# A two-block transformer kernel on one core: first tiles through token blocks together, a centring matrix in the value turn, one filler stream for the last pair

## What is computed

```python
h = rms_norm(x, norm_mix_g)
proj = h @ w_in
slab = proj[..., :RWKV_COLS]; slab = slab + (shifted(slab) - slab) * mu      # token shift
r, k, v, wd, ad, gd = split(slab)
decay = exp(-exp(-softplus(-(w0 + tanh(wd) @ w2)) - 0.5))
a = sigmoid(a0 + ad @ a2);  g = sigmoid(gd) @ g2
kk = k * k_k / norm_of_head(k * k_k)
y = delta_rule_scan(r, decay, k, v, -kk, kk * a)      # linear in v
y = (y - mean_of_head(y)) * rsqrt(var_of_head(y) + GN_EPS)
mix = (y * lnx_g + lnx_b + bonus(r, k, v)) * g
x = x + concat([mix, memory_attention]) @ w_out
```

## Time and profile before

| | |
|---|---|
| median of 3 runs (1564.57 to 1568.79) | 1567.27 us |
| the profiled execution's own time | 1571.59 us |
| its span, first to last instruction | 1569.8 us |
| mean granted TensorE clock | 0.987 |
| PE busy | 95% of the span |
| DVE / ACT / POOL busy | 52% / 36% / 16% |
| chain that ended last: PE / DVE / ACT / issue | 81% / 9% / 5% / 3% |
| DMA, mean | 81 GB/s |

### The profile page before, as it was taken

How to read it: one execution, slowest core, us unless ns; L and a number is a source line. 1 busy time by engine, 2 the same in 40 slices (tenths; PEclk the granted TensorE clock), 3 DMA queues, 4 the chain that set the end, 5 groups by cost and what they waited for, 6 DMA issues and landing times.

```text
span 1569.8 us, 26697 instructions
## 1 busy us (share of the span) xinstructions
PE 1486.0 (95%) x11374; PEld 1165.1 (74%) x11374; DVE 821.5 (52%) x1275; ACT 561.1 (36%) x931; POOL 257.8 (16%) x183
## 2 busy tenths in 40 slices
PE   6889998887799999999999999999989999999999
PEld 4666766665588888888878876666768888888887
DVE  6556555665455354453564348688564443444343
ACT  6443344445142222221353337554434331222131
POOL 3133332320020000000020002222322220120120
PEclk9999999999999999999999999999999999999999
DMA  6221101120023323232222232221222333232323
GB/s 217 68 69 43 30 29 29 34 77 3 28 81 94 101 87 108 82 106 94 94 83 93 81 101 88 90 82 58 68 81 94 94 94 108 81 108 94 94 84 104
DMA packets 38517, 127.67 MB, mean 81 GB/s; under 512 B 4224, under 2 KB 5248, under 8 KB 38400
## 3 DMA queue, kind: packets, MB, share of 16 engines
q1 hardware_dynamic: 38400, 125.97, 25.5%
HBM read 123.86 MB, written 2.10 MB: 80 GB/s over the span
## 4 chain that ended last, share of the span: by engine, by line
PE 81%; DVE 9%; ACT 5%; issue 3%; POOL 1%; DMA 0%; SPq 0%; POOLq 0%; DVEq 0%; ACTq 0%
PE bank L927 78%; PE bank L1327 1%; ACT Whi L1967 1%; DVE qa L1640 1%; DVE Hlo L1530 1%; ACT slab L2020 1%; PE bank L1042 1%; DVE Wlo L1524 1%; DVE ftmp L1583 1%; DVE slab L1585 0%; DMA x<-in_xT 0%; PE bank L1117 0%; DVE qa L1638 0%; ACT slab L2152 0%; ACT L2071 0%
## 5 line engine op out<-in xcount | busy, mean ns | idle before, releaser
L927 PE MATMUL bank<-Hhi,Whi 128*128 128x512 f32 x912 | 377.8, 414 | 18.1 <-DVE Wlo L1524 10.3
L927 PE MATMUL bank<-Hhi,Wlo 128*128 128x512 f32 x912 | 364.2, 399 | 0.0
L927 PE MATMUL bank<-Hlo,Whi 128*128 128x512 f32 x912 | 362.3, 397 | 0.0
L927 PE MATMUL bank<-Uhi,Whi 128*128 128x512 f32 x736 | 291.3, 396 | 9.5 <-DVE Ulo L1820 4.0
L927 PE MATMUL bank<-Ulo,Whi 128*128 128x512 f32 x736 | 287.3, 390 | 0.0
L927 PE MATMUL bank<-Uhi,Wlo 128*128 128x512 f32 x736 | 287.3, 390 | 0.0
L1967 ACT CAST Whi<-Wraw 128x1024 fp32r<-128x1024 f32 (+1 forms) x216 | 223.2, 1037 | 161.0 <-PE bank L927 147.0
L1524 DVE TENSOR_TENSOR Wlo<-Wraw,Whi 128x1024 fp32r<-128x1024 f32 (+1 forms) x177 | 226.9, 1282 | 99.9 <-ACT Whi L1967 99.8
L927 PEld LDWEIGHTS bank<-Hhi,Whi 128*128 128x128 f32 x912 | 173.4, 190 | 76.3 <-issue 12.7
L927 PEld LDWEIGHTS bank<-Hlo,Whi 128*128 128x128 f32 x912 | 173.2, 190 | 42.1
L927 PEld LDWEIGHTS bank<-Hhi,Wlo 128*128 128x128 f32 x912 | 173.8, 191 | 34.2
(11 more groups left out here) (302 smaller groups left out, 1638.0 us busy)
## 6 DMA issues: line engine op xcount, KB each, us to landing
Wraw<-in_wts SPq DMA_DIRECT2D x208, 512.0 KB, 3.5
bA<-in_biasA SPq DMA_DIRECT2D x12, 256.0 KB, 2.8
Wraw<-in_wts SPq DMA_DIRECT2D x8, 384.0 KB, 3.2
x<-in_xT SPq DMA_DIRECT2D x8, 256.0 KB, 4.4
X<-in_xT SPq DMA_DIRECT2D x2, 1024.0 KB, 7.2
out<-X SPq DMA_DIRECT2D x8, 256.0 KB, 2.1
bB<-in_biasB SPq DMA_DIRECT2D x4, 384.0 KB, 3.0
memX<-in_memT SPq DMA_DIRECT2D x2, 512.0 KB, 7.0
```

The lines of the kernel that those rows point to most:

```text
L927: return e.matmul(o, lhsT, rhs, start=start, stop=stop, skip_group_check=True)
```

## The change

- Start: x blocks drive three tiles at once (`wa`, `gd`, slab k of pair 0), each tile catching up when its weights are there; weight units 1 and 2 are split inside the loop, so the loads of units 3 and 4 (which wait for Wlo of units 0 and 1) stand ahead of x blocks 2 and 3 in SP's order, and the constants go behind x block 5. The sums of squares of x and of the memory move from POOL to DVE. Two of the ring's banks serve as tile banks for the third and fourth tile. The token-shift's second half becomes a step of its own (`shift`), one tile late in the start.
- The sigmoid of `gd` is a Tanh (scale 0.5) on ACT and an affine on POOL.
- Values less their mean: `turn_v` multiplies by the matrix `cent` (identity less the head's mean) instead of transposing; the `mean` step (matmul and DVE subtraction) is gone, `gsq` squares y at once.
- `table(f)`: a 128x1 activation of function f ahead of the wait in `root` (kinds x, f, t) and in `sg`.
- In `ahead`, exponentials come before the key norm's `root`. Of the 256-column tiles (km) the spreading `hn` comes one flush later. In `mem_projections` the memory's `root` comes after the first qm tile.
- The low part Ulo is a step `tlo` after `tg`. Filler rates: pairs 1.5 to 1.35, pair 0 1.1 to 1.05, room after `sb` 0.7 to 1.4.
- Last pair: `inverse(5)`, `states(5)`, `tail(5)` are one main strand with one filler stream at rate 0.93: bonus, `states(4)`, `tail(4)` in turns with all of the memory attention, then the 14 w_out steps. POOL keeps making Wlo till that strand ends.

```diff
-FILL_FRONT, FILL_TAIL = 0.2, 1
-FILL_PAIR = (1.1, 1.5, 1.5, 1.5, 1.5, 0.87)
+FILL_FRONT, FILL_LAST = 0.2, 0.93
+FILL_PAIR = (1.05, 1.35, 1.35, 1.35, 1.35)
...
+    firsts = [tile(kind, key, ("rw", m), "x", range(8))
+              for kind, key, m in (("wa", (18,), 18), ("gd", (19,), 19), ("slab", (0, 1), 6), ("slab", (0, 0), 0))]
+    first_norm = norm(("x",))
     for i in range(8):
         x0.take(("x", i))
         step("xload", i)
-        if i < 2:
+        if i < 3:
             loads(i + 1)
-        if i == 3:
+        if i == 5:
             step("cload")
+        step("x", i)
+        count("Hlo", "x", i)
+        if i < 3:
+            splits(i + 1)
...
+        step("xq", i)
         x0.give(("x", i))
...
+        for n, g in enumerate(firsts[0:3]):
+            for _ in range(i + 1 if i == n else i > n):
+                next(g)
+            if i == 7 and n == 0:
+                splits(4)
+                next(first_norm)
     step("memload")
+    splits(5)
+    for _ in range(4):
+        next(firsts[3])
+    run(first_norm)
+    state["held"] = held = []
+    for n, g in enumerate(firsts):
+        run(g)
+        if n:
+            shift(held[n - 1])
+        if n == 2:
+            splits(6)
+    shift(held[3])
...
         yield next(r)
+        step("exps", p)
+        step("kf", p)
         bank("root", "f", p)
         yield 0.9
-        step("exps", p)
-        step("kf", p)
...
         two("sb", p)
-        yield 0.7
+        yield 1.4
...
     def tail(p):
-        bank("mean", p)
-        yield 1.0
+        step("gsq", p)
         yield 0
         bank("root", "t", p)
...
         bank("tg", p)
+        yield 1.0
+        step("tlo", p)
         count("Ulo", "mix", p)
-        yield 1.0
+        yield 0
...
+    def beside():
+        yield from turns(itertools.chain(bonus(NP - 1), states(NP - 2), tail(NP - 2)), mem_att)
+        step("Xload")
+        for g in outs:
+            yield from spaced(itertools.islice(g, 7), 0.8)
+
+    filler = beside()
+    blend(itertools.chain(inverse(NP - 1), states(NP - 1), spaced(tail(NP - 1), 1)), filler, FILL_LAST)
+    run(filler)
     state["lo"] = "wlo"
...
         def turn_v(p):
             w.wait_ge(S["shift"], N("shift", slab_tile[p, 2]))
-            transposes(("vn", p), lambda cp: v_[:, 128 * cp:128 * cp + 128]).then_inc(S["vn"])
+            b = bank("vn", p)
+            for cp in range(4):
+                x = mm(b[:, 128 * cp:128 * cp + 128], v_[:, 128 * cp:128 * cp + 128], c("cent"), True, True)
+            x.then_inc(S["vn"])
...
+        def token_square(i):
+            if i:
+                w.wait_ge(S["xsq"], i + 1)
+                w.wait_ge(S["xadd"], i - 1)
+                e.tensor_tensor(acc[:], acc[:], ftmp_of(("x", i))[:], ALU.add).then_inc(S["xadd"])
...
+        def table(function):
+
+            w.wait_ge(S["C"], 16)
+            e.activation(spare[:], c("rmseps"), function, scale=1.0)
```

More of the change, by code:

```diff
@@ L186, in make_plan @@
     plan.TC = late = Slots(4)
-    state = {"loads": 0, "splits": 0, "units": 0, "lo": "wlo"}
+    state = {"loads": 0, "splits": 0, "units": 0, "lo": "wlo", "ahead": 1, "held": None}
     pend = []
@@ L212, in unit @@
         state["units"] += 1
-        splits(u + NW - 1)
+        splits(u + state["ahead"])
         return u
@@ L329, in make_plan @@
             ftmp.give(("x", i))
-        step("x", i)
-        count("Hlo", "x", i)
+        step("xq", i)
         x0.give(("x", i))
-        if i == 0:
-            splits(1)
-    splits(2)
-    step("memload")
-    around(tile("wa", (18,), ("rw", 18), "x", range(8)), tile("gd", (19,), ("rw", 19), "x", range(8)),
-           norm(("x",)))
+        for n, g in enumerate(firsts[0:3]):
[4 more added lines that the diff above has]
+                next(first_norm)
+    step("memload")
+    splits(5)
[10 more added lines that the diff above has]
+    shift(held[3])
+    state["held"] = None
+    for t in (2, 3):
+        M.give(("first", t))
+    state["ahead"] = NW - 1
     def mem_norm():
@@ L504, in make_plan @@
     early = turns(normed, rates0())
[L505 removed]
+    weave(itertools.chain(*(spaced(projection(0, i), 2) for i in (2,))), early, 1.5)
     run(early)
@@ L1989, in root @@
             r = N("root", kind, *key)
+            if kind in ("x", "f", "t"):
+                table(ACT.Sqrt)
             w.wait_ge(S["root"], r)
@@ L2050, in evict, with shift @@
                 e.copy(Hhi2[:, x.key[1], :], tmp_of(("sig", t - 1))[:]).then_inc(S["uphi"])
+        def shift(t):
+            kind = tiles[t].kind
+            if kind == "slab":
+                return
+            w.wait_ge(S["shift"], N("shift", t))
+            if kind == "wa":
+                e.activation(WA[0:64, :], WA[0:64, :], ACT.Tanh, scale=1.0).then_inc(S["lora"])
+            else:
+                e.activation(GD[:], GD[:], ACT.Tanh, scale=0.5).then_inc(S["lora"])
         def gained(ver, i):
@@ L2471, in constants @@
     put("ident", np.eye(128))
+    put("cent", np.eye(128) - same / 64.0)
     put("mneg", -1.0 * (s < t))
```

136 lines of the change are left out of this document (65 added, 71 removed).

## The result

The changed kernel takes 1573.11 us (median of 20 runs, 1568.22 to 1577.88), the kernel before 1567.91 us (20 runs, 1563.93 to 1575.59). The ratio is 1.0031, with a 95% interval of 1.0018 to 1.0044: slower by some 5 us, where 22.5 us less were forecast. So the two profiles are as long as each other, and what they show side by side understates the loss by about 5 us; I compare stretches, and leave whole times to the runs.

The account below looks back on a forecast made before the run. PE bounds it, busy 95% of the span; only its idle time ahead of 430.6 us can move. Start 10, pairs 4 and last pair 8.5 give 22.5 us off 1567.3: 1544.8, range 1531 to 1561.

Parts of the forecast that it names:

- (b): Pairs 0 to 4: `tn` comes 1.4 us earlier, so PE's waits for the gate step's product go, 3.9 us off.
- (a): Pairs 0 to 4: four means go (4.0 us) and five turns of v grow (2.5), 1.5 us off.
- (c): Pairs 0 to 4: the wait for `sb`'s last eviction, 8.1 us in five, stays.
- (d): Pairs 0 to 4: requesting Tanh ahead can't cut the decays' waits; `root` behind exponentials costs pair 2 1.4 us.
- The start: Start and memory projections: fourth tile ends at 38 us, memory's root at 54 to 57; 10 us off, bounds 0 and 16.
- The last pair: Pair 5 as one stream without pair 4's and 5's means: 8.5 us off, bounds 14 and -2.
- the net 1.5 of the first part: Last pair, first part: 2 off for the mean, 1.9 for the last level's wait, 2.4 charged for memory attention rounds.
- The second part: Last pair, second half: memory attention rounds and pair 5's mean leave, w_out steps move behind the last wait; 7.0 us off.
- The dense rest: From 430.6 us on: unchanged, only starting earlier or later; a change over 2 us would show the prediction wrong.
- Slower: starved levels: Rival, chance 0.08: with less filler per unit, level steps wait for their evictions, 25 us more, 1570.
- Tables matter: Rival, chance 0.07: the small activations pull each table load out of the wait for the decays, 1538.

Follow-up runs that it names:

- e2: Changed kernel with `ops` one couple of matmul steps earlier, so that it stands ahead of `tn` again: 1561.09 us, 0.9938 of the kernel before.
- e13: Kernel before with one `yield 0` of the tail left out, so the written order becomes `tn`, `ops`, last couple: 1580.42 us, ratio 1.0073.
- e5: Changed kernel with `ops` ahead of `tn` again and Tanh's table requested behind the eviction of `kn`: 1553.59 us, 0.9907 of the kernel before.
- e3: Changed kernel with the request for Tanh's table moved from `sg` to behind the eviction of `kn`: 1563.98 us, 0.996 of the kernel before.
- e6: Kernel before with one 128x1 Tanh activation added behind the eviction of `kn`: 1558.85 us, ratio 0.9951.
- e1: Changed kernel with the tail's yield after `gsq` put back from 0 to 1.0: 1575.9 us, 1.0036 of the kernel before.
- e7: Changed kernel with three unused products of constants ahead of `sb` in pairs 2 to 5, keeping PE busy: 1573.38 us, 1.0032 of the kernel before.
- e10: Changed kernel with the key norm's `root` ahead of the exponentials again: 1570.53 us, 1.0004 of the kernel before.
- e11: Changed kernel with one tile instead of three going along with the x blocks: 1576.41 us, 1.0049 of the kernel before.
- e8: Changed kernel with the last pair written as before, two blends one after the other: 1579.94 us, 1.0063 of the kernel before.
- e4: Changed kernel with the pairs' filler rates and the room after `sb` put back as before: 1569.51 us, 0.9995 of the kernel before.

## Why the prediction was wrong

- **The step that failed** is (b) of pairs 0 to 4: "`tn` now comes ahead of the last couple of matmul steps ..., 3.9 off". It does come ahead of that couple, but of `ops` too, which stood between; I followed the order on PE and counted 1.4 us gained, and did not lay out DVE's queue. There, the three products of `ops` now stand between `tn` and the gate product, POOL's share of `tn` runs beside two of them, and each takes 1.07 us longer. The wait went from 0.98 to 3.26 us instead of to nothing. e2 and e13 put the price at 12 to 13 us, e5 against e3 at 10.4, the waits themselves at 9.2; against the 3.9 of gain, that is a miss of 13 to 16 of the 27.7 between forecast and result. The forecast also gave the pairs' clock no term: PE was to be busy 1.8 us less over pairs 0 to 4 (four means less, 0.45 more for each of five turns), and is busy 3.7 more, at 0.93 where it was 0.96.
- **(a)** The mean's product went, and turns with `cent` take 0.89 us instead of 0.44 (I had 0.5 more). The size held as PE work, but not as a gain: with the mean gone, `root` t waits 0.81 us for ACT's square in each of pairs 1 to 4 (L2200, 3.2 us in all). No pair of before, e6 or e13 has such a wait. So 3.2 of the four means' 4.0 us come back. In e1, where a yield of 1.0 again stands between the square and `root`, the wait is gone, but the time isn't less: others had come in. The prediction took the product's time off and didn't ask what the fillers at its yield of 1.0 had covered.
- **(c)** said that the wait for `sb`'s eviction stays. It fell to 4.1 us, and this was no gain: PE reached it later and at the lower clock (e7, where it is 9.1 again).
- **(d)** held, and was right on both sides. The request for Tanh in place helps nothing: its load stands right behind the cast, and the waits are as long. Pair 2's decays got a load more, 1.99 for 0.51 us; e10 gives 2.6 us for it (not clear of noise), where I had 1.4. What I missed is that the request is worth 8 to 9 us when it is placed where ACT idles (e3, e6). The rule on tanh beside exp in one set, of the Trainium skill ("ScalarE: Activation LUTs"), agrees with both kernels: before, pair 2's decays come behind exponentials without a load; in the changed kernel, no load stands between the loads at 148.45 and 154.10 us, where the decays and the exponentials are. Its price of 2.66 us for a switch, with a drain, did not come up: load and activation take 1.28 and 0.20 us in the rows of e3, one 0.01 us behind the other, and by 2.66 the wait that e10 takes out would have grown by nearly twice the 1.41 that it did (0.58 to 1.99).
- **The start** gave 6.5 of 10. The waypoints were close: the fourth tile ends at 36 (38), the memory's root starts at 55.85 (54 to 57), with a tile before it. The root came 1.8 us later than before (I had 0.8), the spreading of km waits 1.1 (I had 0). I put the rest, 1.4 us, down to the qm tile: the low clock behind the root's wait, which slowed it before, now slows the tile that comes there, so that 24 x 0.23 = 5.5 us went and not 7.6. That would be 2.1, and wasn't tried; the scatter of the starts (82.8 to 84.5) is as large. That the four tiles' gain goes into the wait for the memory's sum (4.39 to 6.11) held, and e11 bears it out by half.
- **The last pair** gave 2.7 of 8.5. That one stream fills holes was right, and e8 gives it 6.8 us, more than the 4.6 that were its part. The term that failed is the net 1.5 of the first part: from the first scores to the wait for the last level it is 3.8 longer (62.1 for 58.3 us). I charged 2.4 for the rounds and nothing for the clock; PE is busy 7.9 more there, at 0.89 for 0.99. The second part is 6.6 us shorter (I had 7.0).
- **The dense rest** is 2.4 us shorter, which passes the 2 us that I had named as a sign of being wrong. Before, PE came to it out of a wait of 4.01 us and was granted 0.59 in the first 4 us; now the wait is 1.46 and the clock there 1.00:

```profile
430.60:434.60 4.00, 4.00 (x11) 3.04 (x12) 2.04 (x3) 1.24 (x2) 0.00 (x0) 0.59 0.00 0
```

```profile
432.70:436.70 4.00, 3.81 (x16) 2.85 (x17) 2.03 (x3) 1.38 (x3) 0.00 (x0) 1.00 0.00 0
```

  That is 4 x 0.41 = 1.6 us. The other three executions with the 4.0 us wait (e6, e8, e13) also have 0.57 to 0.60 there, and take 1136.1 to 1139.0 us for the rest; so what is left of the 2.4 is within the scatter.

- **The rivals.** "Slower: starved levels" had the sign, with 0.08, and not the mechanism: no level step of pairs 1 to 4 shows a wait of 0.5 us or more. "Tables matter" was right that a load can be pulled out of that wait, but not by this change. The changes sum to -6.5 + 11.3 - 2.7 - 2.4 = -0.3 us in the profiles. Of the 5.2 us between the medians, about 5 are the distance of the profiled runs from their medians (3.7 above, 1.6 below), which no stage shows. By the runs, the parts are: order of `tn` and `ops` +12, root behind the exponentials +2.6, single stream -6.8, three tiles instead of one -3.3. That is +4.5, near the 5.2; but each part is known to some 2 to 4 us only, so the sum proves little. The products less the mean, the squares' additions on DVE and `hn` one flush later were not tried alone.

## What to carry to other kernels

Where strands are woven by weights, a part that is taken away moves all that follows: print the order of the steps on every engine before and after, and look for pairs that changed places on a queue that isn't the one you cut. A product that releases POOL doesn't belong in front of two-input products on DVE, when the next release hangs on them. And a table is to be asked for where ACT idles, not just ahead of its use; one 128x1 activation moved so was worth 8 to 9 us, where the whole change with its order mended gave 7 (e2 against before).

A step that looks like pure cost can cover another: look what waits where it stood (the fillers written behind the mean's product covered ACT's square). And a profile is one execution: here two with equal length belonged to kernels 5 us apart.

## What the runs showed of the hardware

- A product of two 128x512 operands in SBUF takes DVE 0.69 us alone and 1.76 us while POOL has one too, and POOL's takes 1.65 or 1.51 instead of 1.27 and 1.29. Where the two overlap only in part, DVE's takes 1.14 or 1.34 (L1756 in e2 and e4). Products with a bank as operand stayed at 0.68 us beside POOL (L1774 before, at 233.02, beside L2350). The Trainium skill ("SBUF — State Buffer", SBUF: two separate sides) has the two engines share a port pair that one of them holds for a whole instruction, on DVE with two SBUF operands; the choice of who is slowed agrees with these rows. So do the sizes: both slow products end some 0.55 us behind the POOL product beside them (234.12 to 233.57, 235.79 to 235.25).
- Behind waits of 3.26 us, and of 1.99 (152 to 156 us), PE was granted 0.57 to 0.64 of the clock over 4 us, in part at its lower level of 1.2 GHz. That cost 1.6 us where PE was the bound (dense rest), 1.1 to 1.3 where the stretch behind the decays' wait was longer (pair 2 against pair 3), and nothing where PE next waited for DVE (e7): a low clock is to be priced by what stands behind it.
- ACT loads a table as soon as it comes to the instruction, ahead of what that instruction waits for, but behind all earlier work on its queue. In the kernel before, the load of the square root stands 5.1 us ahead of its activation, which then waits 3.83 us for PE:

```profile
152.79 1.28 ACT L1997 ACT_TABLE_LOAD   x1
157.91 0.18 ACT L1997 ACTIVATE st<-bank 128x8 f32<-128x8 f32 x1 [3.83 <-PE bank L927]
```

So a load is free where ACT is idle before the work arrives, and a request right ahead of its user gains nothing where ACT was busy until then.
